# First projection tile of a two-layer trunk: two quarters interleaved chunk by chunk with the narrow gate projection, their high parts made earlier and the low parts spread over other engines

## The reference

```python
def trunk_layer(x, cvec, p, lam_init, ctx):
    shift1, scale1, gate1, shift2, scale2, gate2 = modulation(cvec, p['w_ada'], p['b_ada'])
    h = rms_norm(x, p['norm1_w']) * (1 + scale1) + shift1
    (mq, mk, mv, mo, mg, nq, nk, nv, dq, dk, dv, sz, sxbc, sdt, gpre) = split_cols(h @ p['w_in'])
    ...
    x = x + gate1 * (mixed @ p['w_out'])
    h2 = rms_norm(x, p['norm2_w']) * (1 + scale2) + shift2
    x = x + gate2 * expert_choice_ffn(h2, p['w_router'], p['w_gate'], p['w_up'], p['w_down'])
```

## Time and profile before

| | |
|---|---|
| median of 3 runs | 1935.22 us (1933.69 to 1942.61) |
| profiled execution: time / span | 1934.42 us / 1932.6 us |
| PE busy | 1743.8 us (90%) |
| DVE, ACT, POOL busy | 636.9, 548.2, 516.5 us |
| chain that ended last | PE 58%, DMA 36%, DVE 3%, ACT 2% |
| HBM traffic | 293 GB/s over the span |

### The profile page before, as it was taken

The page is one execution under the profiler, slowest core; times in us unless marked ns, Lnnn a source line. Parts: engine busy times, 40 slices in busy tenths (PEclk is TensorE's granted clock), DMA queues, the critical chain, the costliest instruction groups (busy, mean ns, idle before and its releaser), DMA issues.

```text
span 1932.6 us, 22632 instructions
## 1 busy us (share of the span) xinstructions
PE 1743.8 (90%) x9126; PEld 1109.4 (57%) x9126; DVE 636.9 (33%) x1387; ACT 548.2 (28%) x1054; POOL 516.5 (27%) x654
## 2 busy tenths in 40 slices
PE   6999999999998788888889999999999978888887
PEld 3888997898532222222268889878965322222223
DVE  3196345873300000001144853568641000001011
ACT  4435453343421011010144444432432111111011
POOL 1787353473100000000047754425820000000000
PEclk9999999999999999999999999999999999999999
DMA  9635434556999999999973364354656999999996
GB/s 357 165 109 188 170 121 152 183 219 247 383 399 428 424 428 427 426 427 425 391 205 131 110 212 157 116 200 159 257 191 260 426 426 426 427 426 427 426 426 272
DMA packets 121512, 567.78 MB, mean 294 GB/s; under 512 B 21824, under 2 KB 31296, under 8 KB 96320
## 3 DMA queue, kind: packets, MB, share of 16 engines
q1 hardware_dynamic: 110624, 543.91, 71.4%
q10 hardware_dynamic: 9920, 20.84, 3.0%
q0 software_dynamic: 864, 1.58, 0.2%
HBM read 550.57 MB, written 15.73 MB: 293 GB/s over the span
## 4 chain that ended last, share of the span: by engine, by line
PE 58%; DMA 36%; DVE 3%; ACT 2%; issue 0%; POOL 0%; ACTq 0%; SPq 0%; DVEq 0%
PE banks L808 31%; PE banks L1383 11%; DMA work<-in_w_gate 8%; DMA ring<-in_w_up 6%; DMA work<-in_w_up 6%; DMA ring<-in_w_down 6%; DMA ring<-in_w_gate 4%; DMA work<-in_w_down 3%; PE banks L814 2%; PE banks L1147 1%; PE banks L1131 1%; PE banks L1352 1%; PE banks L845 1%; ACT work L1488 1%; DMA ring<-in_w_branch 1%; DMA work<-in_x_sample 1%
## 5 line engine op out<-in xcount | busy, mean ns | idle before, releaser
L749 POOL TENSOR_TENSOR ring_fp32r<-ring,ring_fp32r 128x256 fp32r<-128x256 f32 x592 | 464.9, 819 | 814.5 <-ACT ring_fp32r L1488 813.7
L1383 PE MATMUL banks<-ring,work 128*64 128x512 f32 x1776 | 403.9, 599 | 76.2 <-DMA ring<-in_w_gate 33.8
L808 PE MATMUL banks<-xT_fp32r,ring_fp32r 128*128 128x384 f32 x1280 | 344.5, 342 | 2.1 <-POOL ring_fp32r L749 1.8
L1488 ACT ACTIVATE work<-banks 32x512 f32<-32x512 f32 (+6 forms) x400 | 202.7, 528 | 435.9 <-PE banks L1383 250.0
L1383 PEld LDWEIGHTS banks<-ring,work 128*64 128x64 f32 x1776 | 123.0, 137 | 335.2 <-issue 203.2
L1383 PE MATMUL banks<-work 128*64 128x512 f32 x972 | 224.1, 597 | 39.8 <-DMA work<-in_w_gate 15.2
L808 PEld LDWEIGHTS banks<-xT_fp32r,ring_fp32r 128*128 128x128 f32 x1280 | 233.1, 188 | 13.5 <-issue 5.0
L808 PE MATMUL banks<-hT_fp32r,ring_fp32r 128*128 128x384 f32 x640 | 214.7, 336 | 0.0
L2416 DVE SCALAR_TENSOR_TENSOR xT<-banks,mod,xT 128x128 f32<-128x128 f32 (+1 forms) x128 | 46.8, 413 | 445.9 <-PE banks L1419 445.6
L1488 ACT ACTIVATE ring_fp32r<-ring 128x1024 fp32r<-128x1024 f32 (+1 forms) x164 | 154.4, 970 | 78.3 <-PE banks L808 67.0
L1383 PEld LDWEIGHTS banks<-work 128*64 128x64 f32 x972 | 67.3, 137 | 178.4 <-issue 111.1
(11 more groups left out here) (302 smaller groups left out, 1681.1 us busy)
## 6 DMA issues: line engine op xcount, KB each, us to landing
ring<-in_w_up SPq DMA_DIRECT2D x38, 2048.0 KB, 30.6
ring<-in_w_gate SPq DMA_DIRECT2D x37, 2048.0 KB, 30.6
ring<-in_w_down SPq DMA_DIRECT2D x36, 2048.0 KB, 30.3
ring<-in_w_in SPq DMA_DIRECT2D x28, 2048.0 KB, 8.4
ring<-in_w_ada SPq DMA_DIRECT2D x20, 2048.0 KB, 8.7
work<-in_w_down SPq DMA_DIRECT2D x20, 2048.0 KB, 30.6
work<-in_w_gate SPq DMA_DIRECT2D x18, 2048.0 KB, 30.5
work<-in_w_up SPq DMA_DIRECT2D x16, 2048.0 KB, 30.6
```

Source lines behind the costliest of these rows:

```text
L749: ins = pool.tensor_tensor(rounded(w_), w_, rounded(hi_), ALU.subtract)
L808: mm = pe.matmul(dst, a_, b_, start=(first and i == 0), stop=(last and i == 2))
L1383: mm = pe.matmul(dst[64 * hf:64 * hf + 64, :], x(k), w[kk][:, 512 * hf:512 * hf + 512], start=(k == 0), stop=(k == KC - 1), tile_position= ...
L1488: return act.activation(dst, src, ACT.Copy, scale=scale)
```

## The change

In both layers TensorE now works off quarters 0 and 1 together with the narrow projection: for each chunk three narrow matmuls, three of quarter 0, three of quarter 1. Layer 1 has 10 `turn_over` matmuls instead of 14. In layer 0 VectorE makes the high parts of quarters 0 and 1, ahead of the amplitudes, and all eight low parts of `hT`. In layer 1 ScalarE makes the high parts of quarters 0 to 2 between the squares of the end of layer 0 and that of quarter 3 ahead of the narrow weights' copy; GpSimd makes the low parts of all four quarters first and then those of chunks 0, 1, 2, 4, 5 and 6; VectorE multiplies three chunks ahead and the other five inside the loop of casts.

```diff
+LOW_ON_POOL = ((), (0, 1, 2, 4, 5, 6))
@@ GpSimd
                 if l:
-                    low_parts(1)
-                for k in range(0, KC, 2):
+                    low_parts(4)
+                for k in LOW_ON_POOL[l]:
                     pool.wait_ge(sem["xh_ready"], 8 * l + k + 1)
@@ TensorE
-                turn_over(4, 14 if l else 5)
+                turn_over(4, 10 if l else 5)
                 pe.wait_ge(sem["wsm_lo"], l + 1)
+                first_two = [quarter(c)[0] for c in range(2)]
                 for k in range(KC):
-                    pe.wait_ge(sem["hl_odd" if k % 2 else "hl_ready"], 4 * l + k // 2 + 1)
+                    name, v = low_ready(l, k)
+                    pe.wait_ge(sem[name], v)
                     mm = three_passes(PS[0:24, 7, 0:T], (WSMH[:, k, :], wsm[:, k, :]), h_in(k), k == 0, k == KC - 1)
...
+                    for c, (w, hi) in enumerate(first_two):
+                        if k == 0:
+                            pe.wait_ge(sem["lo_ready"], NQ * l + c + 1)
+                        mm = three_passes(PS[:, c, 0:T], (hi[:, k, :], w[:, k, :]), h_in(k), k == 0, k == KC - 1)
...
-                feature_major()
+                feature_major(2)
@@ ScalarE
+                if l:
+                    high_parts(4)
                 act.wait_ge(par_in[1], 48 * (l + 1))
                 copy(rounded(WSMH), wsm[:, :, :]).then_inc(sem["wsm_hi"], 1)
-                if l:
-                    high_parts(1)
                 act.wait_ge(sem["amp_ready"], l + 1)
                 modulate(l, 0)
+                act.wait_ge(sem["hi_ready"], NQ * l + 2)
                 high_parts(4)
...
                         squares(k)
+                        if k % 2 and k > 2:
+                            high_parts_of(l + 1, (k - 1) // 2)
                     root(l + 1, 0)
@@ VectorE
-                    for k in range(KC):
+                    for k in range(KC if l == 0 or which else 3):
                         TTo(hT[:, k, :], xT[:, k, :], RSTD, ALU.mult).then_inc(sem["hx_ready"], 1)
...
                 if l == 0:
                     modulated(0)
+                    dve.wait_ge(landed[LANDING[("mix", 0, 0)][0]], LANDING[("mix", 0, 0)][1])
+                    for q in range(2):
+                        w, hi = quarter(q)[0]
+                        dve.tensor_copy(rounded(hi), w).then_inc(sem["hi_ready"], 1)
                     first_amplitudes()
...
                 for k in range(KC):
+                    if l and k + 3 < KC:
+                        TTo(hT[:, k + 3, :], xT[:, k + 3, :], RSTD, ALU.mult).then_inc(sem["hx_ready"], 1)
                     dve.wait_ge(sem["h_ready"], 13 * l + k + 1)
                     dve.tensor_copy(rounded(HH_IN[:, k, :]), hT[:, k, :]).then_inc(sem["xh_ready"], 1)
-                    if k % 2:
+                    if k not in LOW_ON_POOL[l]:
```

More of the change, by code:

```diff
@@ L253, with low_ready @@
 SPILLED = 24
+LOW_ON_POOL = ((), (0, 1, 2, 4, 5, 6))
+def low_ready(l, k):
+    own = LOW_ON_POOL[l]
+    if k in own:
+        return "hl_ready", sum(len(p) for p in LOW_ON_POOL[:l]) + own.index(k) + 1
+    return "hl_odd", sum(KC - len(p) for p in LOW_ON_POOL[:l]) + sum(j not in own for j in range(k + 1))
 SEMS = ["ada_part", "ada_evac", "ada_sel", "proj_out", "proj_evac", "gpre_out", "xT_out", "xT_evac", "c_ready",
@@ L880, in h_in @@
                     return HH_IN[:, k, a:b], hT[:, k, a:b]
-                turn_over(4, 14 if l else 5)
+                turn_over(4, 10 if l else 5)
                 pe.wait_ge(sem["wsm_lo"], l + 1)
+                first_two = [quarter(c)[0] for c in range(2)]
                 for k in range(KC):
-                    pe.wait_ge(sem["hl_odd" if k % 2 else "hl_ready"], 4 * l + k // 2 + 1)
+                    name, v = low_ready(l, k)
+                    pe.wait_ge(sem[name], v)
                     mm = three_passes(PS[0:24, 7, 0:T], (WSMH[:, k, :], wsm[:, k, :]), h_in(k), k == 0, k == KC - 1)
-                mm.then_inc(sem["gpre_raw"], 1)
-                banks, po, quarters = (0, 1, 2, 3, 7), [0], [0]
+                    if k == KC - 1:
+                        mm.then_inc(sem["gpre_raw"], 1)
+                    for c, (w, hi) in enumerate(first_two):
+                        if k == 0:
+                            pe.wait_ge(sem["lo_ready"], NQ * l + c + 1)
+                        mm = three_passes(PS[:, c, 0:T], (hi[:, k, :], w[:, k, :]), h_in(k), k == 0, k == KC - 1)
+                        if k == KC - 1:
+                            mm.then_inc(sem["proj_out"], 1)
+                banks, po, quarters = (0, 1, 2, 3, 7), [2], [2]
                 def out_bank():
@@ L905, in next_quarter, with feature_major @@
                     return [(hi, w) for w, hi in quarter(q)]
-                def feature_major():
-                    for c in range(4):
+                def feature_major(first=0):
+                    for c in range(first, 4):
                         b = out_bank()
@@ L1536, in _, with high_parts_of @@
                 ada_take(0, i + 1)
-            for l in range(L):
-                split = [0]
-                def high_parts(until):
-                    while split[0] < until:
-                        q = split[0]
-                        split[0] += 1
+            split = {0: 2, 1: 0}
+            def high_parts_of(l, until):
+                    while split[l] < until:
+                        q = split[l]
+                        split[l] += 1
                         for i in tiles_begun(q):
@@ L1556, in high_parts @@
                         ins.then_inc(sem["hi_ready"], 1)
+            for l in range(L):
+                def high_parts(until):
+                    high_parts_of(l, until)
+                if l:
+                    high_parts(4)
                 act.wait_ge(par_in[1], 48 * (l + 1))
                 copy(rounded(WSMH), wsm[:, :, :]).then_inc(sem["wsm_hi"], 1)
-                if l:
-                    high_parts(1)
                 act.wait_ge(sem["amp_ready"], l + 1)
                 modulate(l, 0)
+                act.wait_ge(sem["hi_ready"], NQ * l + 2)
                 high_parts(4)
@@ L1906, in modulated @@
                     dve.wait_ge(dve_step, step())
-                    for k in range(KC):
+                    for k in range(KC if l == 0 or which else 3):
                         TTo(hT[:, k, :], xT[:, k, :], RSTD, ALU.mult).then_inc(sem["hx_ready"], 1)
-                    dve.wait_ge(sem["hx_ready"], 16 * l + 8 * (which + 1))
+                    if which:
+                        dve.wait_ge(sem["hx_ready"], 16 * l + 16)
                 if l == 0:
                     modulated(0)
+                    dve.wait_ge(landed[LANDING[("mix", 0, 0)][0]], LANDING[("mix", 0, 0)][1])
+                    for q in range(2):
+                        w, hi = quarter(q)[0]
+                        dve.tensor_copy(rounded(hi), w).then_inc(sem["hi_ready"], 1)
                     first_amplitudes()
```

## The result

| | before | after |
|---|---|---|
| median | 1935.4 us, 20 runs (1932.89 to 1942.61) | 1941.03 us, 20 runs (1936.73 to 1945.17) |
| profiled execution: time / span | 1934.42 / 1932.6 us | 1941.47 / 1939.6 us |
| PE, DVE busy | 1743.8, 636.9 us | 1746.3, 647.3 us |
| end of the first tile, layer 0 | 69.20 | 71.18 |
| last expert product to end of the first tile, layer 1 | 52.25 us | 53.76 us |

The ratio of the changed kernel to the one before is 1.0021, with a 95% interval of 1.0013 to 1.0030: 4.1 us more (2.5 to 5.8). (The medians are 5.6 us apart and the means, 1936.12 and 1940.38, 4.3; I go by the ratio.) The forecast was 1.8 us more, within the 0.5% that counts as no change. The changed kernel is measurably slower, but by little. All executions compared here are fast ones, except one of 3540.13 us in experiment 3, which its ratio leaves out.

The account below looks back on a forecast made before the run. The prediction took TensorE's matmuls (mixing) and weight transfers (experts) to bound the kernel, and followed waits at each layer's first tile. Layer 0's +2.8 and layer 1's -1.0 made +1.8 us on 1935.22: 1937.0, range 1931 to 1943.

Parts of the forecast that it names:

- the loss in layer 0: Layer 0's first tile: end of quarter 1 2.8 us late, bounds 0.5 early to 5.0 late.
- the wrong sign: Layer 1's first tile: end of quarter 1 forecast 1.0 us early, bounds 2.7 early to 0.7 late.
- the high bound of the prediction's own sum: Both layers' late bounds together, 5.0 and 0.7, make +5.7 us, 1940.9.
- rival 3: VectorE queues behind GpSimd, in layer 1 at the last residual updates; +8.6 us, 1943.8; chance 0.14 for 1941 and above.
- the first (pieces at 0.71 and the clock up): Interleaved stream absorbs the stall, GpSimd's pieces stay at 0.71 us, clock stays up; -3.2 us, 1932.0; chance 0.17.
- Rival 2: Layer 0's first weight tile lands earlier and doesn't bind; quarter 1 ends 6.4 us early, 1925.9 to 1927.8; chance 0.06.
- The landing at 42.1: Layer 0: first weight tile, issued at 24.70, takes 17.4 us to transfer; VectorE's first high part waits for it.
- the ring cast: Layer 0: VectorE's high part of a weight quarter, about 1.0 us, the first waiting idle from 34.6 to about 42.1.
- the amplitudes: Layer 0: VectorE's two small operations that ScalarE's modulation waits for, forecast at 45.1, 6.0 us later than before.
- The slow stretch: Layer 0: TensorE's stream runs partly at the lower clock after idling, charged at 1.7 us.
- VectorE waits before its reciprocal: Layer 1: ScalarE's fourth high part delays the narrow weights' copy, +1.04 us; reciprocal starts at 987.8 instead of 985.70.
- the same price on the clock: Layer 1: TensorE idle for 3.3 us before its stream, then at the lower clock, charged at 1.7 us.

Follow-up runs that it names:

- experiment 3: Changed kernel, but in layer 1 VectorE makes the narrow weights' low part after the reciprocal and three multiplications; 1938.94 us, ratio 1.0013 to the kernel before.
- experiment 1: Changed kernel with only layer 0's part of the change, layer 1 as before; 1939.57 us, ratio 1.0023 to the kernel before.
- experiment 4: Changed kernel, but in layer 0 VectorE makes the amplitudes before waiting for the first weight tile; 1941.16 us, ratio 1.0022 to the kernel before.
- experiment 9: Changed kernel, but layer 0's first weight tile is issued ahead of the copy of xT to memory; 1934.38 us, ratio 0.9994 to the kernel before.
- experiment 6: Changed kernel with 18 instead of 10 filling matmuls (turn_over) in layer 1; 1938.80 us, ratio 1.0022 to the kernel before.
- experiment 7: Changed kernel with layer 0 as before; in layer 1 experiment 3's move and 16 filling matmuls instead of 10; 1933.91 us, ratio 1.0000 to the kernel before.
- experiment 8: Changed kernel with experiment 5's layer 0, and in layer 1 experiment 3's move and 16 filling matmuls; 1937.03 us, ratio 1.0008 to the kernel before.
- experiment 10: Experiment 9 plus, in layer 1, experiment 3's move and 16 filling matmuls instead of 10; 1933.95 us, ratio 0.9988 to the kernel before.
- experiment 11: Experiment 10 with 11 instead of 5 filling matmuls in layer 0; 1932.70 us, ratio 0.9983 to the kernel before.
- experiment 2: Changed kernel with only layer 1's part of the change, layer 0 as before; 1934.26 us, ratio 0.9999 to the kernel before.
- experiment 5: Experiment 4, but in layer 0 only quarter 0 is interleaved with the narrow projection, quarter 1 following; 1940.63 us, ratio 1.0031 to the kernel before.

## Why the prediction came out as it did

It said 1937.0, within 1931 to 1943, and 0.92 for no change beyond 0.5%. The median is 1941.03. The ratio makes it 4.1 us, 2.3 more than forecast. The direction and the loss in layer 0 were right. Layer 1 had the wrong sign. So the forecast of no change held, by a range 12 us wide against a miss of 2.5 us in layer 1: there the number fitted by the width of the range and not by the mechanism. The median lies 0.1 above the high bound of the prediction's own sum (1940.9), at the lower edge of rival 3. Of the rivals, the first (pieces at 0.71 and the clock up) and the second (an earlier landing) are out by the chain above: 0.87 a piece, two slow stretches, landing at 42.07. (Rival 2's better end is 1935.22 - 6.4 - 2.7 = 1926.1, not 1925.9; nothing hangs on it.)

**Layer 0: right in mechanism and nearly in size.** The landing at 42.1 bound, as measured at 42.07. VectorE waited in front of the ring cast, the amplitudes came 5.6 late (6.0 forecast), and the stream with both quarters ran from 49.88 (50.4 forecast). The slow stretch cost 1.35 (1.7 forecast). Together that is +2.0 instead of +2.8 in this execution; experiments 1 and 4 have 2.7 and 3.7. One emphasis was wrong: I let the amplitudes' delay look like a cost of its own, and experiment 4 shows that it costs nothing beside GpSimd's eight pieces. It wasn't far from it: in the changed kernel the first six matmuls, begun at 47.58 behind the late modulation, waited only 0.22 for the pieces. Experiment 9 confirms the root of it, by moving the landing.

**Layer 1: the step that failed.** It is "VectorE waits before its reciprocal", where I took the narrow weights' low part at its old cost and set the reciprocal's start at 987.8, 2.1 later than before. Counted from the last expert product, to set two traces on one time base:

| from the last expert product (us) | before | forecast | after |
|---|---|---|---|
| root starts | 19.2 | 20.2 | 20.15 |
| narrow weights' copy starts | 19.7 | 21.8 | 21.6 |
| reciprocal starts | 20.3 | 22.4 | 24.9 |
| stream starts | 29.0 | 28.5 | 31.1 |
| end of tile | 52.25 | 51.2 | 53.76 |

(The forecast's numbers are its 985.6, 987.8, 993.9 and 1016.6 less 965.37, and for the copy 19.7 and twice 1.04. The stream of before is counted from its first narrow matmul, 994.39.) Up to the copy the forecast holds to 0.2. Then the subtraction takes 2.98 instead of 0.36, and these 2.6 stay to the end: the stretch came out 2.5 above the forecast. Both profiles of the table have the slow stretch at the updates, so it cancels between them. The idle time before the stream was 5.83 instead of 3.3, with the same price on the clock, 1.6 against the 1.7 that I charged; experiment 6 shows that this price is real. The reason I gave for it was weaker than it looked: the idle time of 2.48 that a slow stretch followed at 974 was followed by none in six of the thirteen profiles. What holds is the comparison at the stream itself: in layer 1 the five profiles with 16 or 18 filling matmuls (6, 7, 8, 10 and 11), idle for at most 1.01 before the stream, take 20.93 to 21.09 for the 120, and the six with 10 (the changed kernel, 2, 3, 4, 5 and 9), idle for 3.77 to 5.85, take 22.62 to 23.65.

The mechanism was on my list, but in the wrong place. Rival 3 had VectorE queue behind GpSimd at the last residual updates. They kept their 0.74 a pair. What queued was the subtraction of the narrow weights, which stood on the path while GpSimd ran sixteen pieces in a row. I had noted the 0.66 of a tiny operation beside GpSimd, and charged it in layer 0, but in layer 1 I had GpSimd at its pieces until 990.7 in one sentence and VectorE past the subtraction at 987.8 in another, and didn't set the two side by side. In the trace after, less the 4.81 by which its experts end later, the subtraction starts at 987.3 and GpSimd ends at 990.1.

The Trainium skill's page "SBUF — State Buffer", section "SBUF: two separate sides", describes the shared port pair as held for one instruction, whoever is first. By that the subtraction would lose at most the rest of one piece, about 0.7, and end after 1.1. The runs measured 2.98 to 3.00 in three profiles, four pieces, and 0.50 to 0.93 in three others. In all three long ones the subtraction ended 0.21 to 0.22 behind GpSimd's last piece. The measurement decides: beside back-to-back pieces the loser can miss several turns, here all that were left. The page allows for the wait, but not for its length.

**The rest of the time goes with the clock, as far as it is known.** The changed stretches sum to +3.5 in this execution, and the ratio says +4.1, so for the changed kernel they agree. Over all twelve kernels the time is on average 1.5 us above what the two yardsticks sum to, most in experiments 5 and 6 (3.2 and 4.8), least in 2 (1.4 below); the 0.9 by which the yardstick of before may be long would be over half of that. The profiler gives the mean granted clock of every execution. It averages 0.9916 over the 20 of the changed kernel, and 0.9947, 0.9951 and 0.9946 over the 35, 30 and 28 of the kernel before that stand beside the experiments. Between executions of the kernel before, and between those of the changed one, 0.001 less goes with 1.4 to 1.7 us more. In the two profiles the kernel before has four slow stretches (near 51, 973, 1450 and 1761), the changed kernel ten: the two entries hold two each (45 to 53 and 998 to 1005), where before the first holds one and the second none, and the other six lie near 492, 513, 977, 1455, 1772 and 1926. So three of the six more lie at the changed entries. An estimate for the mean execution: in those windows one slow stretch adds up to 1.7 us of missing clock, and 0.0031 of 1940 us is 6.0, which makes three to four more slow stretches, about as many as the changed entries have. That leaves little for the code that wasn't changed. It is a comparison of averages and not an experiment, and what experiments 5 and 6 lost beyond their stretches stays open.

## What to carry to other kernels

Before an operation is moved to an idle engine, look up when its data lands, not when it was first read: here a transfer that nobody waited for had 4 us to spare for its old reader, and held the new one, which was there 8.6 us before it landed. A subtraction on VectorE that stands on the path should not meet a long unbroken run on GpSimd: put it where that run is over, or price it at all that is left of the run. Where a stream starts after some idle time, filling matmuls up to its start cost less here than the slow stretch that they saved, even when they ended a little late (experiments 6 and 11). And when single traces are compared, look for slow stretches inside the yardstick first.

## What the runs showed of the hardware that I had not expected

- The same 128x192 subtraction on VectorE took 0.36 alone, and in layer 1 0.50, 0.92, 0.93, 2.98, 2.98 and 3.00 beside GpSimd's pieces; in layer 0, also beside them, 0.34 or 0.35 in the changed kernel and in experiments 1, 3, 6, 9, 10 and 11, and 0.88 in experiments 4, 5 and 8. In layer 0 eight pieces took 6.96 (0.87 each) while VectorE's other operations took 0.63 to 0.97: both lost a little. In layer 1 sixteen took 11.01 (0.69 each) where the subtraction lost everything, and 11.12 or 11.13 where it got in. I can't say what decides between the two.
- The reciprocal isn't touched: 2.55 us in experiment 3, wholly beside GpSimd's pieces, and 2.55 in layer 0 of the kernel before (at 28.18), where GpSimd was idle.
- With 36 filling matmuls up to the start of the stream there was no slow stretch (granted clock 1.00, 20.93 us for 120); with 20 and 5.83 us of idle time there was one (0.57, 22.62). An idle time alone doesn't decide it: behind the same 2.48 at the end of layer 0 the granted clock fell to 0.50 in seven profiles and stayed at 1.00 in six.
- A transfer of 2 MB took 17.4 to 18.0 us behind a 1.5 MB store on the same queue, and 13.2 to 13.8 ahead of it; the store then took 17.0 to 17.2 instead of 11.5 to 13.3.
- Executions of the same instructions differ by up to 7 us between the two entries. The number of slow stretches in between goes with it: none in the shortest, five in the two longest.
